# First matrices, tokens and column vectors handed over in the order in which they are loaded, without transposes on TensorE

## The chip, the cores and the metric

The kernel runs on one core of one Trainium2 chip. Its time is the device time of one execution in microseconds, and the lower the better. Several executions are timed, and one more is recorded by the hardware profiler.

The engines: PE (TensorE, matrix products; PEld is its weight load), DVE (VectorE), ACT (ScalarE), POOL (GpSimd) and SP (SyncE, which here only issues DMAs). Sixteen DMA engines move data between HBM and SBUF. Matrix products write to PSUM.

## The reference, cut to what matters

Two transformer blocks on 256 tokens of width 1024, in float32. The first block has two layers. Its beginning is what matters here: a modulation vector is made of the condition, tokens and context are scaled and shifted by it, and then projected.

```
def adaln_params(cond, w_mod, b_mod):
    m = jax.nn.silu(cond) @ w_mod + b_mod          # (1024) @ (1024, 6144)
    return jnp.split(m, N_MOD, axis=-1)

def modulate(h, shift, scale):
    return h * (1 + scale) + shift

sh1, sc1, g1, sh2, sc2, g2 = adaln_params(c, w_mod[i], b_mod[i])
csh1, csc1, ... = adaln_params(c_ctx, w_mod[i], b_mod[i])
hx = modulate(x, sh1, sc1)                          # x: (256, 1024)
hc = modulate(h_ctx, csh1, csc1)                    # ctx: (256, 1024)
q_l = apply_rope(hx @ w_qkv[:, :1024])              # queries of the tokens
k_c, v_c = project_kv(hc, w_qkv)                    # keys and values of the context
k_l, v_l = project_kv(hx, w_qkv)                    # and of the tokens
...                                                 # attention, output projection, gate
x = layer_norm(ALPHA * x + g1 * y_lat, ln_g, ln_b)  # the residual needs x again
...                                                 # feed-forward, second layer, second block
```

Further vectors (gains and offsets of the norms) scale single columns of later activations.

## The kernel before, in words

One core computes everything. The order of work is written out by hand, engine by engine (`@block.sync`, `.gpsimd`, `.scalar`, `.vector`, `.tensor`); engines wait for each other by counting semaphores, and each engine runs its list in order.

**Weights.** A matrix is cut into pieces ("subs") of 128 x 1024. SP loads two subs at a time into `raw` (6 buffers of 2048 columns). For each sub n, `adv(n)` on ACT (L707) copies `raw` to `wH`, the part that TensorE's fast float32 form keeps, and `adv(n)` on DVE (L1268) subtracts it from `raw` to `wL`, the rest. Activations are split in the same way into `aH` (ACT) and `aL` (DVE), for the context `cH` and `cL`. A product is three matrix products (`three`, L2141 to L2143, of 512 columns; `columns_T`, L2178 to L2180, of 256): high x high, high x low, low x high.

**The first stage** is where the change lies. It goes in four steps m = 0 to 3, each for 256 of the 1024 columns of the tokens:

- SP issues per step (L493 to L501) the modulation matrix's columns into `mod0` (two DMAs of 1 MB), 256 columns of the tokens into `x` (256 KB), and the first two query chunks' rows into `raw` (two of 512 KB). Then it issues the context into `ctxr` (1 MB), the first key chunk, the rest of the constants (L506), and the other chunks as buffers come free.
- ACT's own queue loads the vectors `c`, `c_ctx`, `b_mod` and `attn_subln_g` as rows of `rows` (L762 to L765), and the first constants with the identity matrix (L766).
- PE begins with `zero_mm(5, 4)`, products of zeros (L2385) that nothing reads, then transposes `rows` (L2391), so that ACT can take the vectors as columns from PSUM (L769 to L772): `cT` (after silu), `subg`, `bcol`.
- `mod_mm(m)` (L2352) multiplies `cT` by the step's modulation matrix. ACT copies the row (`mod_copy`, L759), `mod_select` (L2362) turns it into columns, `mod_put` on DVE (L1327) adds `bcol`: `modcol`.
- `x_group(m)` transposes the step's tokens (four transposes, L2328). `hi_x` on ACT (L779, L781) modulates them from PSUM into `tf` and copies them to `aH`; DVE (L1389) makes `aL`.
- `q_mm(c, s)` (12 products each) multiplies them by query chunk c = 0, 1. PE's order interleaves this: 12 products of `q_mm(0, s)` and 3 of `q_mm(1, s)` come ahead of `mod_mm(s+1)`, the rest of `q_mm(1, s)` between `mod_mm` and `mod_select` and behind it. Two `zero_mm(2, 5)` stand in the first step, one in the third.
- `ctx_group(0)` to `(3)` do for the context what `x_group` does, two around the last query chunks and two behind the first key sub; `hi` with `mod` (L721, L724) and `low_ctx` (L1280) make `cH` and `cL`.

**What follows** is `chunk_mm` for keys and values (subs 8 to 23), attention, and all other projections, each sub with the same `adv` on ACT and DVE ahead of it. `beside_qkv` puts steps of further modulation vectors (`vec_steps`, fed by POOL's loads into `modraw`) and `rotate` (rotary embedding) on DVE into the key and value chunks. POOL's third load of this kind waits until the context's transposes are done, as `ctxr` lies in the same memory.

**The gains.** Much later, POOL loads twelve small vectors as rows (L625 to L635), PE transposes them in `o_last` (L2534), and ACT copies them to `gcol` (L899 to L901).

Of the kernel before, what the change touches and what calls it, by code (L numbers as in the profile page):

```python
# [33 lines left out]
P = 128  # L34
# [48 lines left out]
for _name, _count in (("x", 4), ("ctx", 4), ("q", 4), ("k", 4), ("att", 16), ("o", 4), ("x1", 4), ("in0", 2),  # L83
                      ("pool", 4), ("x3", 4), ("in1", 2), ("rms0", 4), ("glaA", 2), ("mqk", 8), ("oa", 4),
                      ("ob", 4), ("y", 4), ("rms1", 4), ("up", 4), ("rms2", 4), ("p", 1)):
    GROUPS[_name] = _n
    _n += _count
# [126 lines left out]
def build(nc, a, cst_d, pool_d, out):  # L214
    ctx = ExitStack()
    with ctx:
# [20 lines left out]
        rows = sb(ctx, "rows", [113, P])  # L237
        rows2 = rows[0:82, :]
# [11 lines left out]
        ctxr = modraw[:, 2:4, :]  # L250
# [6 lines left out]
        ro = lnp[:, :, :].rearrange("p u (t c) -> p u t c", t=TT)  # L257
        modrow = sb(sA, "modrow", [P, 512])
# [3 lines left out]
        bcol = sb(sA, "bcol", [P, 96])  # L262
# [120 lines left out]
        ctx_in, rows_in, cst_in, cst2_in = (sem(n) for n in ("ctx_in", "rows_in", "cst_in", "cst2_in"))  # L383
# [8 lines left out]
        rows_T, cT_zero, cT_ready = sem("rows_T"), sem("cT_zero"), sem("cT_ready")  # L392
# [13 lines left out]
        rows2_in, rows2_T, gcol_ready = sem("rows2_in"), sem("rows2_T"), sem("gcol_ready")  # L406
# [62 lines left out]
        def _(sp):  # L469
# [23 lines left out]
            for m in range(NMOD0):  # L493
                for w in range(2):
                    sp.dma_start(mod0[:, 2 * m:2 * m + 2, :].rearrange("p h (k c) -> p (h k) c", k=4)[:, :, 256 * w:256 * w + 256],  # L495
                                 by_k(a["w_mod"][0])[:, :, w * D + 256 * m:w * D + 256 * m + 256]).then_inc(mod0_in[m], 16)
                cols = slice(256 * m, 256 * m + 256)
                sp.dma_start(x[:, :, cols], a["x"].rearrange("b (t p) d -> p (b t) d", p=P)[:, :, cols]).then_inc(x_in[m], 16)  # L498
                for c in range(2):
                    sp.dma_start(raw[:, m, c * D:(c + 1) * D].rearrange("p (k c) -> p k c", k=2),  # L500
                                 by_k(a["attn_w_qkv"][0])[:, 2 * m:2 * m + 2, c * CW:(c + 1) * CW]).then_inc(w_raw[m], 16)  # L501
            sp.dma_start(ctxr[:, :, :], a["ctx"].rearrange("b (t p) d -> p (b t) d", p=P)).then_inc(ctx_in, 16)
            for c in range(2, 6):
                chunk(SUBS["qkv"] + 4 * c, a["attn_w_qkv"][0], c * CW)
                if c == 2:
                    sp.dma_start(cst[:, C_DIST:C_END], cst_d[:, C_DIST:C_END]).then_inc(cst2_in, 16)  # L506
            rows_of(SUBS["wo"], a["attn_w_o"][0], 0, KT)
# [40 lines left out]
        def _(pool):  # L548
# [29 lines left out]
            def vec_load(v):  # L578

                layer, m = VECS[v]  # L580
                for k in range(KT):
# [14 lines left out]
                    elif n == 2:  # L596
                        pool.wait_ge(t_done, GROUPS["ctx"] + 4)
# [27 lines left out]
            for j, nm in enumerate(("norm_mix_2", "norm_mlp_2", "norm_ple_2")):  # L625
                pool.dma_start(rows2[8 * j:8 * j + 8, :], a[nm].rearrange("l (r p) -> (l r) p", p=P))\
                    .then_inc(rows2_in, 16)
            pool.dma_start(rows2[24:32, :], a["gla_out_norm_2"].rearrange("l h (r p) -> (l h r) p", p=P)).then_inc(rows2_in, 16)
            pool.dma_start(rows2[32:33, :], a["moba_k_norm_2"]).then_inc(rows2_in, 16)
            pool.dma_start(rows2[33:34, :], a["moba_q_norm_2"]).then_inc(rows2_in, 16)  # L630
            for j in range(6):
                w = (a["ln_g"], a["ln_b"])[j % 2]
                k = (0, 2, 3)[j // 2]
                pool.dma_start(rows2[34 + 8 * j:42 + 8 * j, :],
                               w[k // 2, k % 2:k % 2 + 1, :].rearrange("l (r p) -> (l r) p", p=P)).then_inc(rows2_in, 16)  # L635
# [54 lines left out]
        def _(act):  # L690
# [66 lines left out]
            def mod_copy(c):  # L757
# [4 lines left out]
            act.dma_start(rows[96:104, :], a["c"].rearrange("b (r p) -> (b r) p", p=P)).then_inc(rows_in, 16)  # L762
            act.dma_start(rows[104:112, :], a["c_ctx"].rearrange("(r p) -> r p", p=P)).then_inc(rows_in, 16)
            act.dma_start(rows[0:96, :], a["b_mod"].rearrange("l (r p) -> (l r) p", p=P)).then_inc(rows_in, 16)
            act.dma_start(rows[112:113, :], a["attn_subln_g"]).then_inc(rows_in, 16)  # L765
            act.dma_start(cst[:, 0:C_DIST], cst_d[:, 0:C_DIST]).then_inc(cst_in, 16)  # L766
            act.wait_ge(rows_T, 1)
            act.wait_ge(cT_zero, 1)
            nc.scalar.activation(cT[:, :, 0:2].rearrange("p k r -> p r k"),  # L769
                                 ps[:, 6, 96:112].rearrange("p (r k) -> p r k", r=2), ACT.Silu).then_inc(cT_ready, 1)  # L770
            nc.scalar.activation(subg[:, 0:2], ps[:, 6, 112:113].to_broadcast([P, 2]), ACT.Copy, scale=1.0 - LAM_INIT)
            nc.scalar.activation(bcol[:, :], ps[:, 6, 0:96], ACT.Copy).then_inc(cT_ready, 1)  # L772
            def hi_x(c, shift, scale):

                g = GROUPS["x"] + c
                act.wait_ge(t_done, g + 1)
                for k in range(2):
                    cols = slice(k * S, (k + 1) * S)
                    link(nc.scalar.activation(tf[:, g % 2, cols], tbank(g)[:, cols], ACT.Identity,  # L779
# [2091 lines left out]
```

## Time and profile before

| | |
|---|---|
| median of three runs | 1114.98 us (1114.4 to 1116.2) |
| profiled execution | 1114.75 us |
| its span, first to last instruction | 1113.0 us |
| granted TensorE clock, mean of the span | 1.000 (of 2.4 GHz) |
| PE busy | 1098.3 us |
| DVE, ACT, POOL busy | 778.5, 585.7, 77.0 us |
| moved by DMA | 236.81 MB, mean 213 GB/s |

A row of the timeline gives start, duration, engine, line, operation, what it writes and reads, the form and the number of merged instructions, and in square brackets the engine's idle time ahead of it and what ended that. Matrix products overlap in the array, so rows of PE start before the one ahead has ended; the distance of two starts is their pace, not the duration shown. A product of plain float32 counts as two in the trace: the five of `zero_mm(5, 4)` are a row x10. The row of a stretch gives busy microseconds and instruction counts for each engine, then the granted clock, the DMA engines' share (over 1 where they work on two transfers at once) and GB/s.

### The profile page before, as it was taken

To read this page: it belongs to the slowest core of one execution; us is meant where nothing else is said; L and a number is where in the kernel's file an instruction comes from. 1 tells how busy PE (TensorE), PEld (TensorE's weight loads), DVE (VectorE), ACT (ScalarE), POOL (GpSimd) and SP (SyncE) were. 2 spreads that over 40 slices of the span, in tenths; PEclk is the share of its full clock that TensorE was granted. 3 is DMA by queue.
4 is the path that set the end of the run, shared out by engine and by line. 5 is a ranking of instruction groups with operands and counts; after the bars stand their busy time and mean duration, and the time that the engine had idled before them with its cause. 6 is when DMAs were issued, how large, how long until landed. Compare 5 with 4: busy or idle time off the path is not lost.

```text
span 1113.0 us, 14759 instructions
## 1 busy us (share of the span) xinstructions
PE 1098.3 (99%) x5962; PEld 914.7 (82%) x5962; DVE 778.5 (70%) x926; ACT 585.7 (53%) x823; POOL 77.0 (7%) x144
## 2 busy tenths in 40 slices
PE   8999999999999999999999999999999999999998
PEld 4698766889998887888888878887888888888887
DVE  2497588889789887877755865455667667774454
ACT  3552367564344446665543777465755366563342
POOL 0011130112221201000000000000000000000000
PEclk9999999999999999999999999999999999999999
DMA  9986850769999964777655787786624445655541
GB/s 328 378 274 241 281 150 8 223 215 315 375 371 343 358 217 162 229 244 237 224 207 136 157 249 158 166 169 142 173 102 152 152 161 217 221 193 192 188 161 38
DMA packets 121237, 236.81 MB, mean 213 GB/s; under 512 B 6265, under 2 KB 61954, under 8 KB 121042
## 3 DMA queue, kind: packets, MB, share of 16 engines
q1 hardware_dynamic: 105696, 183.84, 52.6%
q0 software_dynamic: 15184, 51.78, 13.6%
q8 instruction: 47, 0.77, 0.3%
q10 hardware_dynamic: 290, 0.26, 0.1%
q14 instruction: 20, 0.16, 0.0%
HBM read 234.77 MB, written 1.09 MB: 212 GB/s over the span
## 4 chain that ended last, share of the span: by engine, by line
PE 93%; DVE 3%; SPq 1%; DMA 1%; ACT 1%; issue 0%; ACTq 0%
PE ps L2141 19%; PE ps L2143 19%; PE ps L2142 19%; PE ps L2211 10%; PE ps L2213 5%; PE ps L2178 4%; PE ps L2179 4%; PE ps L2180 4%; PE ps L2328 3%; PE ps L2501 1%; PE ps L2463 1%; DMA mod<-in_w_mod 1%; DVE wL L1268 1%; SPq L495 1%; PE ps L2759 0%; SPq L498 0%
## 5 line engine op out<-in xcount | busy, mean ns | idle before, releaser
L1268 DVE TENSOR_TENSOR wL<-raw,wH 128x1024 fp32r<-128x1024 f32 x326 | 394.9, 1223 | 206.5 <-ACT wH L707 204.0
L707 ACT ACTIVATE wH<-raw 128x1024 fp32r<-128x1024 f32 x326 | 339.8, 1058 | 292.8 <-PE ps L2143 199.5
L2141 PE MATMUL ps<-wH,aHL 128*128 128x512 f32 x576 | 229.6, 399 | 2.3 <-DVE aHL L1689 0.9
L2142 PE MATMUL ps<-wL,aHL 128*128 128x512 f32 (+1 forms) x592 | 229.1, 387 | 0.0
L2143 PE MATMUL ps<-wH,aHL 128*128 128x512 f32 x576 | 224.9, 391 | 0.0
L2211 PE MATMUL ps<-aHL,wH 128*128 128x512 f32 x480 | 167.1, 394 | 0.0
L2141 PEld LDWEIGHTS ps<-wH,aHL 128*128 128x128 f32 x576 | 108.2, 188 | 34.5 <-issue 7.3
L2213 PE MATMUL ps<-aHL,wL 128*128 128x256 f32 x480 | 133.4, 278 | 0.0
L2142 PEld LDWEIGHTS ps<-wL,aHL 128*128 128x128 f32 x592 | 111.5, 188 | 20.6
L2143 PEld LDWEIGHTS ps<-wH,aHL 128*128 128x128 f32 x576 | 108.2, 188 | 23.2
L2211 PEld LDWEIGHTS ps<-aHL,wH 128*128 128x128 f32 x480 | 90.1, 188 | 20.7
L2213 PEld LDWEIGHTS ps<-aHL,wL 128*128 128x128 f32 x480 | 90.3, 188 | 0.0
L2178 PE MATMUL ps<-aHL,wH 128*128 128x256 f32 x288 | 82.1, 285 | 0.0
L2180 PE MATMUL ps<-aHL,wL 128*128 128x256 f32 x288 | 81.6, 283 | 0.0
L2179 PE MATMUL ps<-aHL,wH 128*128 128x256 f32 x288 | 81.6, 283 | 0.0
L1354 DVE SCALAR_TENSOR_TENSOR g2b<-modraw,cT,g2b 128x1024 f32<-128x1024 f32 x55 | 70.5, 1281 | 2.9 <-DMA modraw<-in_w_mod 1.6
L2141 PE MATMUL ps<-wH,hH 128*128 128x512 f32 x176 | 69.0, 392 | 0.0
L2143 PE MATMUL ps<-wH,hL 128*128 128x512 f32 x176 | 68.6, 390 | 0.0
L2142 PE MATMUL ps<-wL,hH 128*128 128x512 f32 x176 | 68.5, 389 | 0.0
L601 POOL DMA_DIRECT2D modraw<-in_w_mod x80 | 42.7, 535 | 347.4 <-DVE g2b L1354 141.6
L2178 PEld LDWEIGHTS ps<-aHL,wH 128*128 128x128 f32 x288 | 55.3, 192 | 1.2 <-issue 0.8
L2179 PEld LDWEIGHTS ps<-aHL,wH 128*128 128x128 f32 x288 | 55.3, 192 | 0.0
(363 smaller groups left out, 1541.7 us busy)
## 6 DMA issues: line engine op xcount, KB each, us to landing
raw<-in_ffn_w_in SPq DMA_DIRECT2D x88, 512.0 KB
modraw<-in_w_mod POOLq DMA_DIRECT2D x80, 512.0 KB, 6.5
raw<-in_w_in SPq DMA_DIRECT2D x32, 1024.0 KB
raw<-in_ffn_w_out SPq DMA_DIRECT2D x22, 1024.0 KB
raw<-in_w_up SPq DMA_DIRECT2D x16, 1024.0 KB
raw<-in_w_down SPq DMA_DIRECT2D x16, 1024.0 KB
mod<-in_w_mod SPq DMA_DIRECT2D x8, 1024.0 KB, 11.9
raw<-in_attn_w_qkv SPq DMA_DIRECT2D x8, 1024.0 KB
```

What stands on the lines that cost most here:

```text
L601: pool.dma_start(modraw[:, n % MT, :], a["w_mod"][layer][k * P:(k + 1) * P, m * D:(m + 1) * D])\
L707: nc.scalar.activation(wHigh(n), raw[:, (n // 2) % RAW, (n % 2) * 1024:(n % 2) * 1024 + 1024], ACT.Copy).then_inc(w_hi, 1)
L1268: V.tensor_tensor(wL[:, n % WL, :], raw[:, (n // 2) % RAW, (n % 2) * 1024:(n % 2) * 1024 + 1024], wHigh(n).bitcast(fp32), ALU.subtract).th ...
L1354: ins = V.scalar_tensor_tensor(out=total, in0=tile, scalar=cT[:, k, 0:1], in1=before, op0=ALU.mult, op1=ALU.add)
L2141: T.matmul(outp, xh, h, start=first, stop=False, skip_group_check=part_of)
L2142: T.matmul(outp, xh, l, start=False, stop=False, skip_group_check=part_of)
L2143: return T.matmul(outp, xl, h, start=False, stop=last_, skip_group_check=part_of)
L2178: T.matmul(dst, h, x_h[:, k, :], start=k == 0 and b % 2 == 0, stop=False, skip_group_check=True)
L2179: T.matmul(dst, h, x_l[:, k, :], start=False, stop=False, skip_group_check=True)
L2180: ins = T.matmul(dst, l, x_h[:, k, :], start=False, stop=k == KT - 1, skip_group_check=True)
L2211: T.matmul(dst, wH[:, slot(n + s), c0:c0 + P], aHL[:, k, :, :].rearrange("p a s -> p (a s)"), start=k == 0, stop=False, skip_group_check=True)
L2213: ins = T.matmul(dst[:, S:2 * S], wL[:, (n + s) % WL, c0:c0 + P], aH[:, k, :], start=False, stop=k == KT - 1, skip_group_check=True)
```

## The change

Arrays are laid out by `kernel()` before the launch (moving only, no arithmetic), so that each DMA reads long runs and arrives in the form in which it is used:

- `mod_first` and `qkv_first`: the first modulation and query matrices, partition by partition, in runs of 8 KB and 4 KB (before: 1 KB and 2 KB). Order and amount of these DMAs stay.
- `x_cols` and `ctx_cols`: tokens and context already transposed. `x_group` and `ctx_group` go. ACT modulates from SBUF (`xT`, in the memory of `lnp`, and `ctxT`). The tokens in their own order, which the residual needs, are loaded once more (1 MB) behind the first key chunk; DVE waits for them (`tokens_in`) at the residual.
- `cols` and `gains`: the vectors as columns, one DMA each. Both transposes, their copies from PSUM and eleven DMA issues of POOL go. `bcol` is now a part of `cols`.
- In the first step `zero_mm(2, 5)` becomes `zero_mm(4, 5)`.
- POOL's wait for the context's transposes becomes a wait for ACT's copies (`c_hi`). `hi_x` and the new `hi_ctx` wait for DVE before they write `tf` again.

Tiles that are allocated behind `rows` (512 bytes of each partition, now `cols` with 452) begin 32 bytes lower, those behind `bcol`, which has no memory of its own now, 416 bytes lower in the first stages.

```diff
             for m in range(NMOD0):
-                for w in range(2):
-                    sp.dma_start(mod0[:, 2 * m:2 * m + 2, :].rearrange("p h (k c) -> p (h k) c", k=4)[:, :, 256 * w:256 * w + 256],
-                                 by_k(a["w_mod"][0])[:, :, w * D + 256 * m:w * D + 256 * m + 256]).then_inc(mod0_in[m], 16)
-                cols = slice(256 * m, 256 * m + 256)
-                sp.dma_start(x[:, :, cols], a["x"].rearrange("b (t p) d -> p (b t) d", p=P)[:, :, cols]).then_inc(x_in[m], 16)
+                for h in range(2):
+                    sp.dma_start(mod0[:, 2 * m + h, :], a["mod_first"][:, m, h, :]).then_inc(mod0_in[m], 16)
+                sp.dma_start(xT[:, 2 * m:2 * m + 2, :], a["x_cols"][:, 2 * m:2 * m + 2, :]).then_inc(x_in[m], 16)
                 for c in range(2):
-                    sp.dma_start(raw[:, m, c * D:(c + 1) * D].rearrange("p (k c) -> p k c", k=2),
-                                 by_k(a["attn_w_qkv"][0])[:, 2 * m:2 * m + 2, c * CW:(c + 1) * CW]).then_inc(w_raw[m], 16)
-            sp.dma_start(ctxr[:, :, :], a["ctx"].rearrange("b (t p) d -> p (b t) d", p=P)).then_inc(ctx_in, 16)
+                    sp.dma_start(raw[:, m, c * D:(c + 1) * D], a["qkv_first"][:, m, c, :]).then_inc(w_raw[m], 16)
+            sp.dma_start(ctxT, a["ctx_cols"]).then_inc(ctx_in, 16)
...
                 if c == 2:
                     sp.dma_start(cst[:, C_DIST:C_END], cst_d[:, C_DIST:C_END]).then_inc(cst2_in, 16)
+                    sp.dma_start(x[:, :, :], a["x"].rearrange("b (t p) d -> p (b t) d", p=P)).then_inc(tokens_in, 16)
...
                     elif n == 2:
-                        pool.wait_ge(t_done, GROUPS["ctx"] + 4)
+                        pool.wait_ge(c_hi, 4)
...
             def hi_x(c, shift, scale):
-                g = GROUPS["x"] + c
-                act.wait_ge(t_done, g + 1)
+                act.wait_ge(x_in[c], 16)
                 for k in range(2):
-                    cols = slice(k * S, (k + 1) * S)
-                    link(nc.scalar.activation(tf[:, g % 2, cols], tbank(g)[:, cols], ACT.Identity,
+                    part_ = tf[:, c % 2, k * S:(k + 1) * S]
+                    at_least(act, xq_lo, 2 * (c - 2) + k + 1)
+                    link(nc.scalar.activation(part_, xT[:, 2 * c + k, :], ACT.Identity,
                                               bias=shift[:, k:k + 1], scale=scale[:, k:k + 1]))
...
+            def hi_ctx(j, shift, scale):
+                if j < 2:
+                    act.wait_ge(xq_lo, 2 * (j + 2) + 2)
+                else:
+                    act.wait_ge(c_lo, j - 1)
+                tmp = tf[:, j % 2, :].rearrange("p (k s) -> p k s", k=2)
+                for k in range(2):
+                    ins = nc.scalar.activation(tmp[:, k, :], ctxT[:, 2 * j + k, :], ACT.Identity,
+                                               bias=shift[:, k:k + 1], scale=scale[:, k:k + 1])
+                link(ins)
+                nc.scalar.activation(cH[:, 2 * j:2 * j + 2, :], tmp, ACT.Copy).then_inc(c_hi, 1)
...
             mod_mm(0)
             mod_select(0)
-            x_group(0)
-            zero_mm(2, 5)
+            zero_mm(4, 5)
             q_mm(0, 0)
```

PE's list begins as follows; g1b holds zeros, modrow is the copied modulation row. Before, with what each row waits for:

```order
L2385 MATMUL ps<-g1b 128x512 x4
L2391 MATMUL ps<-cst,rows 128x113 [waits rows_in,cst_in]
L2352 MATMUL ps<-mod,cT 32x512 [waits mod0_in0,cT_ready]
L2352 MATMUL ps<-mod,cT 32x512 x7
L2362 MATMUL ps<-cst,modrow 128x2 [waits mod_row]
L2362 MATMUL ps<-cst,modrow 128x2 x3
L2328 MATMUL ps<-cst,x 128x128 [waits x_in0]
L2328 MATMUL ps<-cst,x 128x128 x3
L2385 MATMUL ps<-g1b 128x512 x2
L2141 MATMUL ps<-wH,aHL 128x512 [waits xq_lo,w_lo]
```

And after:

```order
L2382 MATMUL ps<-g1b 128x512 x4
L2349 MATMUL ps<-mod,cT 32x512 [waits mod0_in0,cT_ready,cst_in]
L2349 MATMUL ps<-mod,cT 32x512 x7
L2359 MATMUL ps<-cst,modrow 128x2 [waits mod_row]
L2359 MATMUL ps<-cst,modrow 128x2 x3
L2382 MATMUL ps<-g1b 128x512 x4
L2138 MATMUL ps<-wH,aHL 128x512 [waits xq_lo,w_lo]
```

Two transposes' places are gone, and the second batch of zero products has four instead of two.

ACT's list at the same place, before:

```order
L762 DMA rows<-in_c 8x128
L763 DMA rows<-in_c_ctx 8x128
L764 DMA rows<-in_b_mod 96x128
L765 DMA rows<-in_attn_subln_g 1x128
L766 DMA cst<-const_tables 128x386
L769 ACT_TABLE_LOAD [waits cT_zero]
L769 ACTIVATE cT<-ps 128x2x8 [waits rows_T]
L771 ACTIVATE subg<-ps 128x2
L772 ACTIVATE bcol<-ps 128x96
L759 ACTIVATE modrow<-ps 128x512 [waits mod_acc]
L707 ACTIVATE wH<-raw 128x1024 [waits w_raw0]
L779 ACTIVATE tf<-ps,modcol 128x256 [waits t_done,mod_out]
```

And after:

```order
L751 DMA cols<-in_cols 128x113
L752 DMA cst<-const_tables 128x386
L755 ACT_TABLE_LOAD [waits cT_zero]
L755 ACTIVATE cT<-cols 128x2x8 [waits cols_in]
L757 ACTIVATE subg<-cols 128x2
L748 ACTIVATE modrow<-ps 128x512 [waits mod_acc]
L696 ACTIVATE wH<-raw 128x1024 [waits w_raw0]
L765 ACTIVATE tf<-lnp,modcol 128x256 [waits x_in0,mod_out]
```

The vectors no longer pass PE, and the tokens are taken from SBUF behind their DMA.

## Rows read from the trace of the kernel before

**Rows 1.** The page, busy time of each engine (share of the span, instructions).

```profile
PE 1098.3 (99%) x5962; PEld 914.7 (82%) x5962; DVE 778.5 (70%) x926; ACT 585.7 (53%) x823; POOL 77.0 (7%) x144
```

**Rows 2.** Waits of PE: who for whom, us in total, times, longest us.

```profile
PE ps L2352 <- DMA mod<-in_w_mod: 2.1, 3, 1.1
```

**Rows 3.** Timeline of PE, start to the second modulation product.

```profile
1.67 6.00 PE L2385 MATMUL ps<-g1b 128*128 128x512 f32 x10 [1.67 <-DVE g1b L1376]
8.74 0.32 PE L2391 MATMUL ps<-cst,rows 113*128 113x113 f32 x1 [1.07 <-DMA cst<-const_tables]
9.86 1.92 PE L2352 MATMUL ps<-mod,cT 128*32 128x512 f32 x16 [0.80 <-DMA mod<-in_w_mod]
...
13.40 0.63 PE L2328 MATMUL ps<-cst,x 128*128 128x128 f32 x4
13.87 1.88 PE L2385 MATMUL ps<-g1b 128*128 128x512 f32 x4
16.03 0.47 PE L2141 MATMUL ps<-wH,aHL 128*128 128x512 f32 x1 [0.27 <-DVE aHL L1389]
...
19.25 1.92 PE L2352 MATMUL ps<-mod,cT 128*32 128x512 f32 x16 [0.22 <-DMA mod<-in_w_mod]
```

**Rows 4.** Timeline of PE, second step to the key chunks, and the gains' transpose.

```profile
25.49 0.47 PE L2141 MATMUL ps<-wH,aHL 128*128 128x512 f32 x1
...
30.22 1.92 PE L2352 MATMUL ps<-mod,cT 128*32 128x512 f32 x16 [1.07 <-DMA mod<-in_w_mod]
...
36.45 0.49 PE L2141 MATMUL ps<-wH,aHL 128*128 128x512 f32 x1
...
40.09 1.92 PE L2352 MATMUL ps<-mod,cT 128*32 128x512 f32 x16
...
46.13 0.47 PE L2141 MATMUL ps<-wH,aHL 128*128 128x512 f32 x1
...
49.31 0.47 PE L2141 MATMUL ps<-wH,aHL 128*128 128x512 f32 x1
...
52.14 0.28 PE L2178 MATMUL ps<-cH,wH 128*128 128x256 f32 x1
...
57.77 1.03 PE L2328 MATMUL ps<-cst,modraw 128*128 128x128 f32 x8
58.56 0.36 PE L2178 MATMUL ps<-cH,wH 128*128 128x256 f32 x1
...
65.06 0.36 PE L2178 MATMUL ps<-cH,wH 128*128 128x256 f32 x1
...
200.84 0.24 PE L2534 MATMUL ps<-cst,rows 82*128 82x82 f32 x1
```

**Rows 5.** Timeline of ACT: two copies of weights that waited for their DMA.

```profile
22.69 1.06 ACT L707 ACTIVATE wH<-raw 128x1024 fp32r<-128x1024 f32 x1 [0.79 <-DMA raw<-in_attn_w_qkv]
...
48.41 1.06 ACT L707 ACTIVATE wH<-raw 128x1024 fp32r<-128x1024 f32 x1 [1.10 <-DMA raw<-in_attn_w_qkv]
```

**Rows 6.** Timeline of DVE: the second step, and the last low halves of the context.

```profile
23.04 0.23 DVE L1327 SCALAR_TENSOR_TENSOR modcol<-ps,bcol 128x4 f32<-128x4 f32 x2 [4.74 <-PE ps L2362]
23.79 1.23 DVE L1268 TENSOR_TENSOR wL<-raw,wH 128x1024 fp32r<-128x1024 f32 x1 [0.51 <-ACT wH L707]
24.93 0.42 DVE L1389 TENSOR_TENSOR aHL<-tf,aHL 128x256 fp32r<-128x256 f32 x1
...
62.28 1.28 DVE L1280 TENSOR_TENSOR cL<-tf,cH 128x512 fp32r<-128x512 f32 x2
```

**Rows 7.** Stretches: runs of 1 KB, of 4 KB, of 2 KB; and behind 70 us.

```profile
2.50:7.50 5.00, 5.00 (x10) 1.93 (x8) 0.00 (x0) 1.28 (x1) 0.00 (x0) 1.00 1.07 350
335.00:340.00 5.00, 5.00 (x44) 5.00 (x44) 4.96 (x6) 2.32 (x4) 1.05 (x2) 1.00 1.03 415
925.00:927.50 2.50, 2.50 (x16) 2.21 (x16) 2.50 (x4) 1.01 (x2) 0.00 (x0) 1.00 1.04 389
70.00:72.50 2.50, 2.50 (x21) 2.29 (x20) 2.38 (x4) 1.47 (x3) 0.53 (x1) 1.00 0.01 4
```

## What the change should do to the time

> **What bounds the kernel now.** I read the page first, then TensorE's waits and its timeline, because one engine is busy nearly all the time: PE works 1098.3 us of 1113.0 [rows 1]. Of what is left, most is at the very start. The first modulation product waits three times for its matrix, 2.1 us together [rows 2], and before the first of them PE stands at a transpose of the vectors, 1.07 us, and at the table of constants that it needs [rows 3]. From the second query chunk on the PE timeline has hardly a gap, so whatever is saved ahead of it should be saved at the end too, unless an engine that feeds PE is as close to its limit. So the question is what sets the pace of the first 58 us. I call the start of the product of `mod_mm(m)` t0 to t3: 9.86, 19.25, 30.22, 40.09 [rows 3, 4]. The steps are 9.39, 10.97 and 9.87 us, and then 12.05 us to the first product with keys, 52.14.
>
> Within a step two things run. One is the DMA: 3.41 MB (2.10 modulation, 0.26 tokens, 1.05 query weights) at 350 GB/s [rows 7] is 9.7 us. The other is a chain: `mod_mm`, its row copied by ACT, `mod_select`, the vector engine's `mod_put`, its low half of the weights, its low half of the activations, and only then the chunk's first product. In the second step that product starts at 25.49, 6.24 us after 19.25, straight after the low half of 24.93 [rows 4, 6]; 15 products of 0.236 us (12 of them take 49.31 to 52.14) come before the next `mod_mm` is due, which makes 9.8 us. DMA and chain are level, and the DMA ends last at t0, t1 and t2.
>
> **The change part by part.**
>
> *Long runs.* The first matrices are read in runs of 8 KB and 4 KB instead of 1 KB and 2 KB, in the same order and amount. The trace has no 8 KB run from this queue. Its bounds: nothing gained (350 GB/s, runs of 1 KB), and 415 GB/s, where runs of 4 KB filled the engines [rows 7]; runs of 2 KB in between gave 389. I take 415, the row nearest in kind. Ahead of the first product lie 2.35 MB (matrix, constants, vectors): 6.7 us at 350, 5.7 at 415, so t0 comes 1.05 us sooner, at 8.8. (PE's zero products end at 7.67, so it can't be before that.) The vectors' transpose goes from this place, but it was hidden behind the matrix and gives nothing by itself. Of later landings, that of the third matrix, 9.16 MB in, comes 4.1 us sooner, at 26.1 instead of 30.22; below I find PE ready for it at 28.2. Only under about 380 GB/s would the DMA pace the steps again.
>
> The Trainium skill says otherwise: "DMA: Bandwidth & Descriptors", section "Where 436 GB/s comes from", lets HBM bind such loads at some 358 GB/s per core, which 350 already nearly is; by that rule this part gives nothing (the first rival below). The rows with 389 and 415 speak against it on this chip.
>
> *Transposes of the tokens go, filler comes.* In the first step PE ran four transposes from 13.40 and two zero products (four rows, 1.88 us) from 13.87, and then waited 0.27 us for the low half until 16.03 [rows 3]. Now four zero products start at 13.40's place. At 0.45 us a row, eight rows last 3.6 us, to t0+7.15, while the chain would have been ready at t0+6.2. With 12 products behind, t1 comes 10.0 us after t0 instead of 9.39: a **loss of 0.6**, t1 = 18.8.
>
> Second step: the transposes (0.4 us) go from PE, and the ACT copy of the weights, which waited 0.79 us for its DMA until 22.69, need not wait any more [rows 5]. What is late next is the vector engine: `mod_put` to t1+4.0, the weights' low half 1.23, the activations' 0.42, with the hand-over some t1+5.85 instead of 6.24 [rows 6]. PE has 9 products until t1+5.8, so they meet. With 15 products 3.54: 9.4 us, t2 = 28.2. Before, with the DMA's wait, it was 10.97: **gain 1.57**.
>
> Third step: PE itself is last here: `mod_select` to t2+3.6 (13.40 lies 3.54 behind 9.86, [rows 3]), six products, one zero product to about t2+5.95, and then the 3.64 us from 36.45 to 40.09 [rows 4]. 9.57 instead of 9.87: **gain 0.30**, t3 = 37.8.
>
> To the first keys: `ctx_group(0)` and `(1)` go; the last chunk starts at t3+5.85 instead of 46.13 (t3+6.04), and 24 products take 5.66 us instead of 6.01 with a group between. 11.51 instead of 12.05: **gain 0.54**. The two groups behind the first key chunk lay from 57.77 to 58.56 with nothing else on PE: **gain 0.79** [rows 4].
>
> *The gains as a table.* One PE transpose goes (200.84, 0.24 us with its drain): **gain 0.15**. POOL loses eleven DMA issues, two ACT copies go; none of them is waited for.
>
> *What is added.* The tokens are loaded a second time, 1 MB behind the first key chunk, some 2.6 us of the SP queue, ahead of the later chunks' weights. From 70 to 72.5 us the queue is empty (4 GB/s, [rows 7]) because all buffers are full, so the megabyte fits there; without that cover it would cost its 2.6 us. The residual waits for it, far later. ACT takes tokens from SBUF instead of PSUM; no row prices that form, I take it at the old one. `cols` is smaller than `rows` and `bcol` goes, so most later tiles begin 32 or 416 bytes lower. No row shows whether an engine minds; I take zero.
>
> *The sum.* 1.05 - 0.6 + 1.57 + 0.30 + 0.54 + 0.79 + 0.15 = 3.8 us. The profiled execution took 1114.75 us, 1.75 more than its span and 0.23 less than the median of the three runs, 1114.98, from which I subtract: **1111.2 us**.
>
> **The rivals.**
>
> *The DMA is no faster* (it is bound by bytes, not runs). Then t0 stays, and t2 stays at 30.22; the loss of 0.6 is hidden in that wait. What remains is 0.30 + 0.54 + 0.79 + 0.15 = 1.8: 1113.2 us. For it: the first 7 us run at 350 with the engines' share over 1. Against it: 389 and 415 at the same share.
>
> *The laid-out arrays read slower.* Partitions of the modulation array now lie 64 KB apart, of the query array 32 KB: powers of two. If neighbouring reads then meet in the same part of the memory, the rate falls. To the fourth matrix there are 12.57 MB. After t3 the gains are 1.48, so the kernel is **slower** once that matrix lands over 1.6 us later than now, that is below some 335 GB/s; at three quarters of 350 it lands 12.1 us later, and the time is 1125.5. Against it: the rows of one weight matrix here lie 16 KB apart and read at 389 [rows 7]. The Trainium skill knows the mechanism ("DMA: Bandwidth & Descriptors", section "Latency and other measured facts"): pitches of 2 and 4 MiB per partition cost copies a quarter and half of their rate, 512 KiB hardly anything; by that, 64 KB would cost nothing. No run shown here has such a pitch.
>
> *The vector engine takes the cover away.* Around 50 to 65 us DVE has no idle time to speak of. Its last low half of the context ends at 63.56, and PE takes the third key chunk at 65.06 [rows 4, 6]: 1.5 us of slack. PE gains 1.33 us between t3 and there. DVE gains too, because the ACT copy at 48.41 waited 1.10 us for a DMA [rows 5] that should now be early. If that does not come, PE waits up to 1.1 us more: 1112.3 us.
>
> **How the numbers follow.** The forecast has 0.66; DMA no faster 0.17; slower reads 0.06; the vector engine's bound 0.08; a start near the bound of 7.7, a microsecond better than I take, 0.03. The range goes from 1109.0 (that start, and the zero products at less) to 1113.5 (the first rival with the scatter of the runs), which leaves out the slow reads and a few accidents. About 0.2%, 2.2 us, is what a measurement can tell from no change here, so faster means under 1112.75: the forecast, the early start and half of the vector engine's case, 0.73. The same: the first rival and the other half, with a little of the slow reads, 0.21. Slower: 0.06.
>
> **What would show it.** The windows from 2.5 to 35 us should show 400 GB/s or more (the first rival: 350; the second: under 335). The first `mod_mm` should start at 8.8 (7.7 to 9.9), without a wait at the second and third. The zero products should run until about 7.1 us after it with no wait behind them; if a wait stands there, they cost nothing. The first key product should start near 49.3 and the second key chunk near 54.9 instead of 58.56, and from there on every PE row should be 3.6 to 3.8 us earlier, to the end. I am wrong if the lead shrinks later: then look at DVE's wait for ACT and at PE's for `cL` between 50 and 70 us, and at the same products' means in the later stages, where the shifted tiles would show.

## The result: slower, although the start gained most of what was foreseen

After the change the kernel takes 1119.47 us (median of six runs, 1119.02 to 1119.97), before it 1114.92 (six runs, 1114.28 to 1116.83): a ratio of 1.0038, 95% interval 1.0028 to 1.0048. The forecast of 1111.2 us and its range, which ended at 1113.5, were wrong, and so was the sign. The profiled execution took 1119.57 us, its span 1117.8.

The page of the changed kernel, busy time of each engine, against [rows 1]:

```profile
PE 1105.3 (99%) x5932; PEld 912.2 (82%) x5932; DVE 778.5 (70%) x926; ACT 585.7 (52%) x820; POOL 71.5 (6%) x133
```

PE has 30 instructions fewer than before and is busy 7.0 us longer. DVE and ACT are where they were. So most of the time was not lost in waiting: PE's products themselves got longer.

First the start. PE's timeline after the change (start, duration, what; in brackets the wait and what ended it), against [rows 3, 4]:

```profile
1.67 7.35 PE L2382 MATMUL ps<-g1b 128*128 128x512 f32 x10 [1.67 <-DVE g1b L1374]
9.17 1.92 PE L2349 MATMUL ps<-mod,cT 128*32 128x512 f32 x16 [0.15 <-DMA cst<-const_tables]
...
12.72 3.68 PE L2382 MATMUL ps<-g1b 128*128 128x512 f32 x8
16.85 0.47 PE L2138 MATMUL ps<-wH,aHL 128*128 128x512 f32 x1 [0.45 <-DVE aHL L1383]
...
19.76 1.93 PE L2349 MATMUL ps<-mod,cT 128*32 128x512 f32 x16
...
29.08 1.92 PE L2349 MATMUL ps<-mod,cT 128*32 128x512 f32 x16
...
38.58 1.92 PE L2349 MATMUL ps<-mod,cT 128*32 128x512 f32 x16
...
49.84 0.28 PE L2175 MATMUL ps<-cH,wH 128*128 128x256 f32 x1
...
55.49 0.28 PE L2175 MATMUL ps<-cH,wH 128*128 128x256 f32 x1
```

The first product with keys starts at 49.84 instead of 52.14, the second key sub at 55.49 instead of 58.56: 3.07 us sooner, where 54.9 was forecast. No modulation product waits for its matrix any more. The stretches of the changed kernel (the last number is GB/s) against [rows 7]:

```profile
2.50:7.50 5.00, 5.00 (x7) 2.02 (x6) 0.00 (x0) 0.89 (x3) 0.00 (x0) 1.00 0.96 391
12.50:40.00 27.50, 27.05 (x141) 16.41 (x140) 10.30 (x18) 12.68 (x20) 0.00 (x0) 1.00 1.02 416
```

Then the rest. I pair the same product in both timelines and take its start after the change less its start before; over 20 us the median of this is the **lead** (negative: sooner). The columns are the stretches that begin at these microseconds of before; above each stands the stage that lies between it and the column to its left (blank: other stages).

| | | values (cH, cL) | | out0 (hH, hL) | in1 (aHL) | out1 (hH, hL) | first of in_w_in | others, oa, up | down (uH, uL) |
|---|---|---|---|---|---|---|---|---|---|
| from, us | 60 | 140 | 340 | 420 | 540 | 600 | 640 | 980 | 1060 |
| changed kernel | -3.12 | -2.25 | -2.44 | -0.52 | -0.74 | +1.14 | +2.02 | +2.54 | +4.81 |

The loss comes in steps, each in a stage whose stationary operand is cH, hH or uH (with its low half): 0.87, 1.92, 1.88 and 2.27 us. Two smaller ones are at 620 us (0.88) and between 800 and 960 (0.5): there some 0.25 go in the products with `oa`, a stationary tile that moved by 32 bytes too, and some 0.2 at the beginning of the up projection, by a pace that experiment 9 is about. In the other stages the lead holds to a quarter of a microsecond. The groups of the page show the same. Before (busy us, mean ns of one):

```profile
L2141 PE MATMUL ps<-wH,hH 128*128 128x512 f32 x176 | 69.0, 392 | 0.0
L2141 PE MATMUL ps<-wH,uH 128*128 128x512 f32 x128 | 49.9, 390 | 0.0
L2143 PE MATMUL ps<-wH,aHL 128*128 128x512 f32 x576 | 224.9, 391 | 0.0
```

and after:

```profile
L2138 PE MATMUL ps<-wH,hH 128*128 128x512 f32 x176 | 70.2, 399 | 0.0
L2138 PE MATMUL ps<-wH,uH 128*128 128x512 f32 x128 | 50.6, 396 | 0.0
L2140 PE MATMUL ps<-wH,aHL 128*128 128x512 f32 x576 | 224.8, 390 | 0.0
```

The same instruction lasts 6 to 7 ns longer with hH and uH, and not with aHL. As the products overlap, the pace (start to start) is the better measure. Two rows 27 products apart, before:

```profile
1039.65 0.39 PE L2141 MATMUL ps<-wH,uH 128*128 128x512 f32 x1
...
1045.77 0.39 PE L2141 MATMUL ps<-wH,uH 128*128 128x512 f32 x1
```

and after:

```profile
1044.26 0.39 PE L2138 MATMUL ps<-wH,uH 128*128 128x512 f32 x1
...
1050.56 0.40 PE L2138 MATMUL ps<-wH,uH 128*128 128x512 f32 x1
```

6.12 us over 27 is 227 ns, 6.30 over 27 is 233. There are 528 products like these with hH and hL, 384 with uH and uL, 96 with cH and cL. These are tiles that the change moved, by 416 bytes (hH, hL, cH, cL) or 32 (uH, uL). aHL, wH and wL did not move.

Two things in the same traces narrow it down. The loads of the stationary tile last as long as before; first before, then after:

```profile
L2141 PEld LDWEIGHTS ps<-wH,hH 128*128 128x128 f32 x176 | 33.1, 188 | 8.0 <-DVE wL L1268 0.8 <-issue 0.4
```

```profile
L2138 PEld LDWEIGHTS ps<-wH,hH 128*128 128x128 f32 x176 | 33.1, 188 | 9.1 <-issue 0.8 <-DVE wL L1266 0.4
```

And the pace does not depend on what else goes on. After the change the products with hH and hL start 234.3 ns apart on average where ACT and DVE are both idle (65 products) and 234.5 where both are busy (175); they start 234.3 ns apart where no DMA packet is under way (102), and also where sixteen or more are (381). So a disturbance by other engines or by transfers is not what slows them.

### The profile page after: what moved, and what is told of

Its sections match the earlier page's. It is cut to its first block, busy times and chain, and to the rows that moved or that the text cites. A ratio compares the mean times of both kernels' runs of the same rounds, so it can differ in the third digit from the quotient of the medians.

```text
span 1117.8 us, 14679 instructions
## 1 busy us (share of the span) xinstructions
PE 1105.3 (99%) x5932; PEld 912.2 (82%) x5932; DVE 778.5 (70%) x926; ACT 585.7 (52%) x820; POOL 71.5 (6%) x133
## 4 chain that ended last, share of the span: by engine, by line
PE 93%; DVE 3%; DMA 2%; ACT 1%; issue 0%; SPq 0%; ACTq 0%
PE ps L2138 19%; PE ps L2140 19%; PE ps L2139 19%; PE ps L2208 10%; PE ps L2210 5%; PE ps L2175 4%; PE ps L2177 4%; PE ps L2176 4%; PE ps L2325 2%; PE ps L2478 1%; PE ps L2444 1%; DMA raw<-in_w_in 1%; DVE wL L1266 1%; DMA raw<-in_qkv_first 1%; PE ps L2349 0%; PE ps L2732 0%
```

## The experiments

The theory is that tiles lie badly. The rivals are the second load of the tokens, the loads' order, or another thing that the change does. Addresses below are in bytes within a partition.

**1. Room for `cols`.** `cols` gets the 512 bytes that `rows` had; the load still fills 113 columns.

```diff
-        cols = sb(ctx, "cols", [P, 113])
+        cols = sb(ctx, "cols", [P, 128])
```

> The changed kernel with one number changed: cols gets 512 bytes of each partition, as rows had, so that every later tile starts at a multiple of 64 bytes again (83 tiles; in the changed kernel 69 start 32 bytes off). Tile-start theory: the lead of 3.1 us that TensorE has at 60 to 80 us stays to the end, products with hH, hL, uH, uL as stationary operand start 227 ns apart instead of 234; 528 x 7.5 + 384 x 7 + 96 x 7 ns and a little for oa make 7.6 us, so 1119.5 - 7.6 = 1111.8 us. Rival (the second load of the tokens, the DMAs' order or the larger pitch lose it later): no change, 1119.5 us.

Measured: 1117.57 us (1115.77 to 1118.67), between the theory's 1111.8 and the rival's 1119.5. Its groups:

```profile
L2138 PE MATMUL ps<-wH,hH 128*128 128x512 f32 x176 | 69.8, 397 | 0.0
L2138 PE MATMUL ps<-wH,uH 128*128 128x512 f32 x128 | 49.9, 390 | 0.0
```

uH, now exactly where it was before the change, has its old pace again (the lead doesn't move in the down projection), hH has not: its products are 232 ns apart. hH starts at a multiple of 64 bytes again, but 384 bytes lower than before, since `bcol` still has no memory. So "a multiple of 64" was too simple a rule. This run showed another loss, of 1.45 us, in in1; it is taken up below.

**2. The kernel before, moved by 32 bytes.**

```diff
+        sb(ctx, "pad", [P, 8])
         gcol = sb(ctx, "gcol", [P, 82])
```

> The kernel before with an unused tile of 32 bytes ahead of gcol: all later tiles start 32 bytes off a multiple of 64, and nothing else changes. Tile-start theory: the same products lose the same 7 to 8 ns each, 7.6 us, so 1114.9 + 7.6 = 1122.5 us. Rival (the loss comes from what the change does, not from where tiles lie): 1114.9 us.

Measured: 1122.72 us (1120.62 to 1122.86). The ratio to before is 1.0056 (1.0041 to 1.007), some 6 us where 7.6 were expected, for an unused tile of 32 bytes. The rival is out: most of what is lost comes from where tiles lie. hH's products lie 233 to 235 ns apart, uH's 232 to 234:

```profile
L2142 PE MATMUL ps<-wH,hH 128*128 128x512 f32 x176 | 70.0, 398 | 0.0
L2142 PE MATMUL ps<-wH,uH 128*128 128x512 f32 x128 | 50.7, 396 | 0.0
```

**3. uH and uL alone.** Experiment 1 with a pad of 32 bytes ahead of uH and one behind uL.

> As the run with cols at 512 bytes, but uH and uL alone start 32 bytes off a multiple of 64 (the tile behind them is put back). If it is the stationary operand's start: 384 products of the down projection, 227 to 234 ns, 2.7 us, and nothing elsewhere: 1111.8 + 2.7 = 1114.5 us. Rival (another tile, for instance what ACT or DVE write or read, or the pattern of all of them together): no loss in the down projection, 1111.8 us.

Measured: 1120.83 us, 3.3 more than experiment 1. In the down projection the lead loses some 2.3 us, 6 ns for each of 384 products; in experiment 1 it lost nothing there. (The other microsecond goes in the stage ahead, up, by the pace that in1 showed in experiment 1.) uH's group, with hH's as in experiment 1:

```profile
L2140 PE MATMUL ps<-wH,hH 128*128 128x512 f32 x176 | 69.8, 397 | 0.0
L2140 PE MATMUL ps<-wH,uH 128*128 128x512 f32 x128 | 50.7, 396 | 0.0
```

**4. hH alone, by 16 bytes.**

```diff
-        hH = sb(sF, "hH", [P, F1 // P, S], f32r)
+        hHw = sb(sF, "hHw", [P, F1 // P * S + 16], f32r)
+        hH = hHw[:, 4:4 + F1 // P * S].rearrange("p (k s) -> p k s", s=S)
```

> As the run with cols at 512 bytes, but hH alone starts 16 bytes off a multiple of 64 (hL stays at a multiple). If a 512-byte row pays for the ninth stretch of 64 bytes that it touches, the 352 products with hH as stationary operand lose the whole 7.5 ns each, 2.6 us: 1114.4 us, and the 176 with hL nothing. Rivals: the loss grows with the offset (half of it, 1.3 us: 1113.1 us); or only 32-byte steps matter (1111.8 us).

Measured: 1117.99 us. Inconclusive as it was meant, for hH was slow already in experiment 1, and hL moved by 64 with it: products with either are 233 to 234 ns apart, against 232.

**5. All old starts.** Experiment 1, and an unused tile where `bcol` was.

```diff
         bcol = cols[:, 16:112]
+        sb(sA, "gap", [P, 96])
```

> The changed kernel with cols at 512 bytes and, where bcol was, an unused tile of its 384 bytes: every tile starts where it started before the change. Theory (it is where the stationary operand starts, and a move of 384 bytes costs too: in the run with cols at 512 bytes uH and uL, unmoved, ran at 227 ns, but hH, hL, cH, cL, moved by 384, at 232): all these products are back at 227 ns, the lead of 3.1 us of 60 to 80 us stays to the end, 1111.8 us; 1113.4 us if the products of the second feed-forward's first matrix take 236 ns instead of 231 again, as they did in that run with operands that had not moved. Rival (the change itself slows the later stages): about 1117.5 us, as with cols at 512 bytes.

Measured: 1113.59 us (1111.96 to 1115.54), a ratio to before of 0.9983 (0.9974 to 0.9992). hH and uH are back:

```profile
L2139 PE MATMUL ps<-wH,hH 128*128 128x512 f32 x176 | 68.9, 392 | 0.0
L2139 PE MATMUL ps<-wH,uH 128*128 128x512 f32 x128 | 49.9, 390 | 0.0
```

The change without its shifts is faster than before. The median is close to the expectation with its clause on in1 (1113.4), in part by luck: the profiled run, 1114.25 us, also loses 0.5 us near 308 us and 0.8 at 620, of which the expectation knew nothing. The lead in the profiled run of each experiment, by stretch:

| from, us | 60 | 140 | 340 | 420 | 540 | 600 | 640 | 980 | 1060 |
|---|---|---|---|---|---|---|---|---|---|
| 1: cols 512 | -3.08 | -2.18 | -2.32 | -0.88 | +0.57 | +2.02 | +2.63 | +2.60 | +2.60 |
| 2: before, 32 bytes | -0.25 | +0.04 | -0.06 | +1.62 | +1.40 | +3.03 | +3.08 | +3.60 | +5.84 |
| 3: uH, uL alone | -3.31 | -2.40 | -2.57 | -1.13 | +0.49 | +1.95 | +2.64 | +3.93 | +6.24 |
| 4: hH by 16 | -3.21 | -2.30 | -2.51 | -0.90 | +0.57 | +2.27 | +3.54 | +3.52 | +3.52 |
| 5: all old starts | -3.48 | -3.48 | -2.98 | -2.99 | -1.31 | -1.27 | -0.45 | -0.36 | -0.36 |
| 6: all 384 on | -3.61 | -2.71 | -2.90 | -1.47 | -1.50 | +0.14 | +0.66 | +0.64 | +0.64 |
| 7: offsets | -3.49 | -3.49 | -2.28 | -0.62 | +1.00 | +2.69 | +3.69 | +4.98 | +6.98 |
| 8: short runs | -0.94 | -0.36 | -0.52 | -0.53 | -0.76 | -0.76 | +0.12 | +0.13 | +0.13 |
| 9: before again | +0.07 | +0.07 | +0.05 | +0.05 | +1.71 | +1.75 | +1.74 | +1.77 | +1.77 |
| 10: split | -3.77 | -3.78 | -2.90 | -2.91 | -2.93 | -2.93 | -2.10 | -2.08 | -2.08 |
| 11: split, two zeros | -4.02 | -4.02 | -4.15 | -4.15 | -4.16 | -4.16 | -3.30 | -3.31 | -3.31 |
| 12: all arrays | -4.40 | -4.40 | -4.08 | -4.08 | -2.44 | -2.40 | -2.44 | -2.42 | -2.42 |

Near 308 us PE waits for a step of DVE's modulation vectors in experiments 5, 7 and 10 (0.44, 0.91 and 0.79 us) and not in the others; no run looks into this.

**6. Is it the address, or the distance to the moving operand?** Experiment 1 with 384 unused bytes ahead of everything: hH is at its old address, but wH and wL, which move through PE while hH stands, are not.

```diff
+        sb(ctx, "pad", [P, 96])
         sLow = ExitStack()
```

> The run with cols at 512 bytes, with an unused tile of 384 bytes ahead of all others: hH, hL, cH and cL are back at their old addresses, but wH, wL, uH, uL and all the rest now lie 384 bytes from theirs. If what counts is the distance between the stationary operand and the moving one (wH, wL), nothing changes: hH and cH products at 232 ns, uH products at 227, 1117.5 us. If it is the address of the stationary operand by itself: hH and cH products 227 ns, uH products 232, 1117.5 - 624 x 5 ns + 384 x 5 ns = 1116.3 us.

Measured: 1117.05 us (1115.21 to 1117.41). The groups are those of experiment 1:

```profile
L2139 PE MATMUL ps<-wH,hH 128*128 128x512 f32 x176 | 69.9, 397 | 0.0
L2139 PE MATMUL ps<-wH,uH 128*128 128x512 f32 x128 | 49.9, 390 | 0.0
```

hH, at its old address, is slow; uH, moved together with wH, is not. The median (1117.05, against 1117.5 and 1116.3 expected) would not have told the two apart; the groups do. It is the **distance** of the two operands. (raw and aHL moved along with wH and wL here. But in the changed kernel the pace was the same whether or not other engines and DMAs were at work, which leaves the operand that PE itself reads.)

**7. Which distances.** Experiment 5 with hH and hL moved by 64 bytes, uH and uL by 128, cH and cL by 256.

> As the run with all tiles at their old starts, but hH and hL 64 bytes further, uH and uL 128, cH and cL 256. The pace of each group's products tells what step costs: with a period of 128 bytes hH is at about 232 ns and uH and cH at 227; with one of 256 only cH is at 227; with 512 or more all three are at about 232. If only the remainder by 64 counts, all are at 227.

Measured (one run): 1121.65 us, and by groups:

```profile
L2142 PE MATMUL ps<-wH,hH 128*128 128x512 f32 x176 | 70.0, 398 | 0.0
L2142 PE MATMUL ps<-wH,uH 128*128 128x512 f32 x128 | 50.6, 395 | 0.0
L2142 PE MATMUL ps<-wH,cH 128*128 128x512 f32 x32 | 12.7, 396 | 0.0
```

64 and 128 bytes cost, 256 does not (cH's group had 12.7 and 396 before, 12.9 and 403 after the change; the lead stays at 3.49 through the values). Of all runs, by distance (start of the stationary tile less that of the moving one) modulo 256: 0: 227 ns; 32: 232 to 235; 64: 233 to 235; 96: 232 to 236; 128: 231 to 232; 144: 233; 192 and 224: 233 to 234. In the kernel before, every stationary tile named here lies at distance 0.

**8. What the long runs are worth.** Experiment 5 with the old DMAs for the first matrices.

> As the run with all tiles at their old starts, but the first modulation and query matrices are read as before the change, in runs of 1 and 2 KB from the arrays as given. If the long runs gave their part of the lead: 350 GB/s instead of 400 to 430 until 40 us, the third modulation product waits for its matrix until about 30 us, the lead at 60 to 80 us is 1.8 us instead of 3.1, and the time 1.3 us more than with long runs. If the transposes that are gone gave all of it: no difference.

Measured: 1116.21 us (1114.53 to 1118.07), 2.6 more than experiment 5. The stretches of this run:

```profile
2.50:7.50 5.00, 5.00 (x7) 2.03 (x6) 0.00 (x0) 1.07 (x3) 0.00 (x0) 1.00 0.99 304
12.50:40.00 27.50, 26.08 (x129) 16.71 (x129) 10.30 (x18) 13.35 (x21) 0.00 (x0) 1.00 1.08 362
```

362 GB/s instead of 416; in the kernel before it was

```profile
12.50:40.00 27.50, 25.94 (x137) 17.04 (x137) 10.33 (x18) 12.44 (x20) 0.00 (x0) 1.00 1.09 359
```

The lead is 0.94, and 0.36 from 71 us on. So of 3.5 us some 3 need the long runs. What else the change does gives 0.4 to 0.9 us while the DMA is as slow as before; what it would give alone, with a DMA that isn't late, this run can't show. Its first matrix even came later than in the kernel before (304 GB/s in the first stretch, against 350).

**9. The kernel before, once more.** It asks where in1's loss comes from.

> The kernel before, unchanged, once more. In the run with all tiles at their old starts, the 480 products of the second feed-forward's first matrix (moving aHL, stationary wH, neither moved) started 236 ns apart instead of 231, 1.55 us in all, though they had their old pace in the changed kernel. If the same instructions fall into one of two paces by chance, the kernel before shows both too: either 231 ns and about 1114.4 us, or 236 ns and about 1116.2 us. If the slower pace comes with the change, this run has 231 ns whatever its time.

Measured: 1116.47 us, with the slower pace. Products of in1, first in the kernel before as profiled at first, then in this run:

```profile
L2211 PE MATMUL ps<-aHL,wH 128*128 128x512 f32 x480 | 167.1, 394 | 0.0
```

```profile
L2211 PE MATMUL ps<-aHL,wH 128*128 128x512 f32 x480 | 168.8, 397 | 0.0
```

The lead differs in in1 alone, by 1.66 us. So the same program has both paces, and in1's loss in experiments 1, 3, 4, 5, 7 and 12 need be no part of the change; experiments 5 and 10, with all tiles at the same starts, show the slower and the faster one. It would also explain why the times of the kernel before come in two groups, near 1114.5 and 1116.3. How often each pace comes was not studied, and it seems to differ between programs: ten of the eleven runs of experiment 1 lie above 1117, one at 1115.77. So the medians hold more or less of it, and the lead by stage is the safer reading.

**10, 11. The first step's chain.** In the changed kernel ACT's first copy of weights waited for both query pieces:

```profile
14.05 1.06 ACT L696 ACTIVATE wH<-raw 128x1024 fp32r<-128x1024 f32 x1 [2.30 <-DMA raw<-in_qkv_first]
```

Experiment 5 with a semaphore for the first piece alone; experiment 11 also has two zero products instead of four.

```diff
...
-                if n % 2 == 0:
+                if n == 0:
+                    act.wait_ge(q_first, 16)
+                elif n % 2 == 0 or n == 1:
...
-            zero_mm(4, 5)
+            zero_mm(2, 5)
```

> The run with all tiles at their old starts, and ACT's first copy of weights waits only for the first query piece (a semaphore of its own), not for both. In the trace of the changed kernel this copy waited 2.30 us, until 14.05; the first piece had landed at 11.88, the second at 13.71. The copy then starts at about 12.2 and the chain to the first query product is ready at about 15.3 instead of 16.85. With the four zero products PE is busy until 16.4, so the product comes 0.4 us sooner and they cost 1.1 us now that their cover is gone: 1113.6 - 0.4 = 1113.2 us. Rival (the next landings, 16.2 to 21.8, set the pace again): the lead at 60 to 80 us is the same as without the split, 1113.6 us.

> As the run with the split wait, with two zero products in the first step, as before the change, instead of four. They end at about 14.6, so the first query product starts at about 15.3, 1.6 us sooner than in the changed kernel, and the lead at 60 to 80 us grows by 1.6 us: 1113.6 - 1.6 = 1112.0 us. Rival (later landings set the pace): as without the split, 1113.6 us.

Measured: 1111.54 us (1111.05 to 1113.92) with four, 1111.98 (1111.18 to 1112.82) with two; both have a ratio to before of 0.9966 (about 0.995 to 0.998). PE with two:

```profile
12.52 1.96 PE L2387 MATMUL ps<-g1b 128*128 128x512 f32 x4
15.20 0.47 PE L2143 MATMUL ps<-wH,aHL 128*128 128x512 f32 x1 [0.72 <-DVE aHL L1388]
...
18.68 1.92 PE L2354 MATMUL ps<-mod,cT 128*32 128x512 f32 x16 [0.52 <-DMA mod<-in_mod_first]
```

The first query product comes at 15.20 as expected, but then the second matrix is the late one. The lead is 4.02, 0.5 more than in experiment 5 and not 1.6: the rival took two thirds. That the median hits the expected 1112.0 is luck, as experiment 5's profiled run, unlike this one, has the slow pace in in1. With four zero products the lead is 3.77: the two more cost 0.25 us once their cover is gone, which the medians are too scattered to show.

**12. The step at 620 us.** In every run with the new set of arrays some 0.85 us go there, in the runs with the old set nothing. ACT waits there for a piece of `in_w_in`, in the changed kernel 2.33 us:

```profile
620.13 2.01 ACT L696 ACTIVATE wH<-raw 128x1024 fp32r<-128x1024 f32 x2 [2.33 <-DMA raw<-in_w_in]
```

Experiment 11, but all old arrays are declared in their old order, used or not, and the new ones behind them.

> As the run with the split wait and two zero products, but all arrays that the kernel before was given are declared again in their old order, used or not, and the newly laid out ones come last. In every run with the new set of arrays, 0.8 us of the lead go at 620 us, where ACT waits for a piece of in_w_in: from 607 to 616 us the DMA moves 150 to 180 GB/s, its 2 KB packets take 136 to 152 ns, while in the runs with the old set it moves 270 to 340 and they take 84 ns. If it is where in_w_in lies in HBM, the packets take 84 ns again, the 0.8 us stay: 1112.0 - 0.8 = 1111.2 us. Rival (it comes from the order of the loads or from the earlier start of that piece): the loss stays, 1112.0 us.

Measured: 1111.76 us (1109.98 to 1113.01). The median alone does not tell the expected 1111.2 from the rival's 1112.0, but the step is gone (-2.40 to -2.44). The stretch 605 to 614 us in experiment 11, then here:

```profile
605.00:614.00 9.00, 9.00 (x44) 7.28 (x43) 7.73 (x9) 6.07 (x13) 0.00 (x0) 1.00 1.01 175
```

```profile
605.00:614.00 9.00, 9.00 (x44) 7.26 (x43) 7.72 (x9) 7.57 (x14) 0.00 (x0) 1.00 1.05 295
```

The load of the same array runs at 295 GB/s instead of 175. An earlier start of that piece isn't the cause: experiment 1 is 2.0 us later there than the kernel before and loses 0.6 us all the same. The profiled run had the slow pace in in1, which may be why the median hardly moves; the two fastest runs, 1109.98 and 1110.20, are the fastest of the study.

## Why the prediction was wrong

**The step that failed** is one clause: the tiles that move by 32 or 416 bytes, "No row shows whether an engine minds; I take zero". It names the unknown and gives it no range; by the prediction's own manner it needed two ends. The stages with moved stationary tiles lost 0.87 + 1.92 + 1.88 + 2.27 = 6.9 us, the step at 620 us, which the prediction did not know at all, 0.88, and the stretch from 800 to 960 some 0.5, which experiment 2 has too (3.08 to 3.60). Less some 0.4 that other stages gave back, that leads from 3.12 us ahead to 4.8 behind. Experiment 5 takes the first part away, experiment 12 the second. The last paragraph of the prediction named the place where this would show, "the same products' means in the later stages", and it showed there.

**The start came near in sum (3.2 us of 3.8) and was wrong in places.** Its terms, predicted and measured from the two timelines:

| | predicted | measured |
|---|---|---|
| first matrix, t0 | +1.05 (8.8) | +0.69 (9.17) |
| zero products, t1 - t0 | -0.6 | -1.20 |
| second step | +1.57 | +1.65 |
| third step | +0.30 | +0.37 |
| to the first keys | +0.54 | +0.79 |
| context's groups behind it | +0.79 | +0.77 |
| gains' transpose | +0.15 | +0.15 |

- t0: the prediction had two bounds, the DMA and PE's zero products, which it took to end at 7.67 as before [rows 3]. They ran until 9.02. The row's wait of 0.15 us behind them ended with the table of constants, which landed after the matrix (8.95) at 9.12. In experiment 5 the zero products ended at 8.43 and t0 was 9.10, so it was the table that held it.
- Zero products: they cost nothing, PE waits 0.45 us for the low half behind them. The loss has the right place and another cause: the chain was not ready at t0+6.2 but at t0+7.7, as ACT waits for the second query piece (14.05 against 13.23 before). Experiments 10 and 11 show it: without that wait and with the four zero products the first step takes 9.91 us, and the prediction had 10.0.
- Second and third step and the keys: right to 0.25 us. The vector engine's rival did not come: no product waits for cL.
- DMA: the windows show 391 and 416 GB/s, where 415 was taken. The rival "no faster" gave 1.8 us for the transposes; experiment 8 shows 0.4 to 0.9. With the DMA at 362 GB/s it again paces the steps, which that sum had left out.
- Slow reads of the laid-out arrays: no sign of it. The Trainium skill's figure for HBM in "DMA: Bandwidth & Descriptors", section "Where 436 GB/s comes from", some 358 GB/s, is passed by the 416 of this trace.

**What stays open.** Why the distance of the operands matters. The two are read at the same time, one product's stationary operand while the other's columns move, as in these rows after the change:

```profile
1045.19 0.39 PE L2139 MATMUL ps<-wL,uH 128*128 128x512 f32 x1
1045.19 0.19 PEld L2140 LDWEIGHTS ps<-wH,uL 128*128 128x128 f32 x1
```

So a conflict of the two reads would fit; but the loads last 188 ns at either pace, and no run looks at the reads themselves. The Trainium skill speaks of a second independent read port for weight loads ("SBUF — State Buffer", section "A bandwidth-pool intuition that's wrong (but worth ruling out)"); 227 against 231 to 236 ns would say, if the conflict is the cause, that here the two are not quite independent. Nor was it tried with products of other types. And why `in_w_in` is read at 175 GB/s with one set of arrays and at 295 with the other was not looked into further; that the arrays lie elsewhere in HBM is a guess.

## What to carry to other kernels

A change that only moves tiles is not free: keep the starts of the stationary and the moving operand of the hot products (here 128x128 stationary, 512 float32 columns moving) a multiple of 256 bytes apart, and when a small tile shrinks or goes, pad it or look at the address of everything behind it. A lead curve (the same product in both timelines) separates at once a gain at the start from a loss later, and a loss by pace from a loss by waiting. In a prediction an effect without a row needs a range, above all where it touches a thousand instructions: 7 ns each were twice the gain that all the other terms were about.

## What was unexpected of the hardware

- The pace of 512-column products depends on the distance of the operands' starts in a partition: 227 ns at multiples of 256 bytes, 231 to 236 at the other distances that came up (experiments 1 to 7). Products of 256 columns with cH and cL as the moving operand keep 120 ns through the change; in experiment 2, at a distance of 32 bytes, they take 116 to 118.
- The same products with the same addresses have two paces by chance: pairs of in1 (512 and 256 columns) take 346 to 347 ns, or 353 in a pattern that repeats every three pairs. It can last the whole stage, 1.6 us in all (experiment 9), or end within it: in the up projection of the changed kernel only the first pairs have it.
- The read rate of an HBM array depends on which other arrays are declared: 175 or 295 GB/s between 605 and 614 us, in the load of `in_w_in` (experiment 12).
- The five zero products at the very start lasted 6.00 us before [rows 3] and 7.35 after, at a granted clock of 1.00 in both; no run looked into why.
